# A hybrid transformer block on one core: the token's norm scale moved behind the input projections, and x loaded in three column pieces

## The reference, cut to what matters

```
h    = x * rsqrt(mean(x*x over channels) + 1e-6) * g_pre_mix     # 256 x 2048
proj = h @ w_in                                                  # 2048 x 20496
m_qk, m_v, m_o, m_if, a_q, a_k, a_v, merge = split(proj)
m_qk = silu(causal_conv4(m_qk) ); gates from m_if + b_gates      # mLSTM branch
attention over a_q, a_k, a_v (ALiBi, block-causal)               # attention branch
mix  = (sigmoid(merge_m) * y_m + sigmoid(merge_a) * y_a) @ w_out
x    = x + rmsnorm(mix);   then an FFN with w_up, conv3, gelu, w_down, and a last norm
```

## Time and profile before

| what | us |
|---|---|
| median of 3 runs | 1852.43 |
| lowest, highest | 1851.65, 1852.64 |
| profiled execution: span, first to last instruction | 1850.7 |
| TensorE busy in it | 1836.6 |
| VectorE, ScalarE, GpSimd busy in it | 1116.1, 899.2, 66.6 |

### The profile page before, as it was taken

The page is one execution under the profiler, slowest core; times in us unless marked ns, Lnnn a source line. Parts: engine busy times, 40 slices in busy tenths (PEclk is TensorE's granted clock), DMA queues, the critical chain, the costliest instruction groups (busy, mean ns, idle before and its releaser), DMA issues.

```text
span 1850.7 us, 35627 instructions
## 1 busy us (share of the span) xinstructions
PE 1836.6 (99%) x13864; PEld 1745.0 (94%) x13864; DVE 1116.1 (60%) x1340; ACT 899.2 (49%) x1174; POOL 66.6 (4%) x92
## 2 busy tenths in 40 slices
PE   8999999999999999999999999999999999999998
PEld 8999999999999999999999889999999999988886
DVE  6666556645665566545555557766667667755555
ACT  6554445444454455444434446555555555544443
POOL 2800000000000000000000000000000000000000
PEclk9999999999999999999999999999999999999999
DMA  7665666566656665666666754666666666665554
GB/s 241 194 192 175 191 182 177 177 188 181 178 172 192 179 176 177 188 193 193 192 192 196 253 198 149 194 193 194 193 193 193 192 194 190 196 215 193 194 193 143
DMA packets 164514, 351.44 MB, mean 190 GB/s; under 512 B 10937, under 2 KB 11473, under 8 KB 163793
## 3 DMA queue, kind: packets, MB, share of 16 engines
q1 hardware_dynamic: 162784, 344.11, 61.1%
q10 hardware_dynamic: 1280, 5.08, 0.7%
q0 software_dynamic: 368, 1.09, 0.2%
HBM read 348.12 MB, written 2.12 MB: 189 GB/s over the span
## 4 chain that ended last, share of the span: by engine, by line
PE 97%; issue 1%; DVE 1%; DMA 1%; ACT 0%; POOL 0%; DVEq 0%; POOLq 0%; SPq 0%; ACTq 0%
PE ps L1348 26%; PE ps L1347 26%; PE ps L1346 26%; PE ps L1563 11%; PE ps L1567 6%; PE ps L1523 1%; PE ps L1427 0%; PE ps L1499 0%; PE ps L1384 0%; DMA gm<-in_channel_rows 0%; DMA raw<-in_w_out 0%; PE ps L1500 0%; ACT ha_hi L631 0%; DVE x L926 0%; PE ps L1506 0%
## 5 line engine op out<-in xcount | busy, mean ns | idle before, releaser
L930 DVE TENSOR_TENSOR w_lo<-raw,w_hi 128x1024 fp32r<-128x1024 f32 x637 | 777.6, 1226 | 640.3 <-ACT w_hi L593 638.2
L593 ACT ACTIVATE w_hi<-raw 128x1024 fp32r<-128x1024 f32 (+1 forms) x641 | 677.7, 1060 | 767.1 <-PE ps L1348 606.9
L1346 PE MATMUL ps<-h,w_hi 128*128 128x256 f32 x3200 | 885.7, 277 | 0.2
L1348 PE MATMUL ps<-h,w_lo 128*128 128x256 f32 x3200 | 884.1, 276 | 0.0
L1347 PE MATMUL ps<-h,w_hi 128*128 128x256 f32 x3200 | 884.1, 276 | 0.0
L1346 PEld LDWEIGHTS ps<-h,w_hi 128*128 128x128 f32 x3200 | 600.9, 188 | 0.9 <-issue 0.6
L1347 PEld LDWEIGHTS ps<-h,w_hi 128*128 128x128 f32 x3200 | 600.8, 188 | 0.3
L1348 PEld LDWEIGHTS ps<-h,w_lo 128*128 128x128 f32 x3200 | 600.7, 188 | 0.0
L1563 PE MATMUL ps<-w_hi,ks_hi 128*128 128x512 f32 x448 | 174.5, 389 | 0.0
L1567 PE MATMUL ps<-w_lo,ks_hi 128*128 128x512 f32 x448 | 174.3, 389 | 0.0
L1563 PE MATMUL ps<-w_hi,ks_lo 128*128 128x512 f32 x448 | 138.1, 389 | 0.0
(11 more groups left out here) (180 smaller groups left out, 1432.4 us busy)
## 6 DMA issues: line engine op xcount, KB each, us to landing
raw<-in_w_in SPq DMA_DIRECT2D x287, 512.0 KB, 3.7
raw<-in_w_up SPq DMA_DIRECT2D x176, 512.0 KB, 4.4
raw<-in_w_down SPq DMA_DIRECT2D x88, 512.0 KB, 4.5
raw<-in_w_branch_m SPq DMA_DIRECT2D x32, 512.0 KB, 4.5
raw<-in_w_branch_a SPq DMA_DIRECT2D x32, 512.0 KB, 4.6
raw<-in_w_out SPq DMA_DIRECT2D x32, 512.0 KB, 4.7
x<-in_x ACTq DMA_DIRECT2D x1, 2048.0 KB, 12.5
gm<-in_channel_rows SPq DMA_DIRECT2D x2, 512.0 KB, 4.6
```

The lines of the kernel that those rows point to most:

```text
L593: return nc.scalar.activation(out_ap, in_ap, ACT.Copy, scale=scale)
L930: nc.vector.tensor_tensor(w_lo[:, at:at + UNIT], raw[:, slot, :], w_hi[:, at:at + UNIT].bitcast(F32), ALU.subtract).then_inc(lo_done, 1)
L1346: nc.tensor.matmul(out_ap, stat_hi, mov_hi, start=start, stop=False, skip_group_check=True)
L1348: return nc.tensor.matmul(out_ap, stat_lo, mov_hi, start=False, stop=stop, skip_group_check=True)
```

## The change

The scale is no longer applied to x. x is loaded in three column pieces of 2, 6 and 8 k-tiles, each with all 256 tokens (256, 768 and 1024 KB), and these loads alternate with the first weight units. TensorE transposes the 128x128 blocks through the identity as before, but of x as it was loaded, with no scale on it. The products of w_in are those of x times gain, and every reader of a w_in chunk multiplies by the token's scale. For channel-major results this is a row of 256 scales, which is made as a product on TensorE (`scales_by_token`) and kept as `rs_row`; for token-major results (v) it is a scalar per partition.

```diff
-            for i in range(len(ROW_PIECES)):
-                sp.dma_start(row_piece(gm_rows, i), x_pieces[i]).then_inc(x_loaded[i], 16)
-            sp.dma_start(wif_flat, by_channel[:, C_ALL:C_ALL + KT * 2 * HEADS]).then_inc(wif_loaded, 16)
+            load_x(0)
             for k, done in ((0, first_loaded), (1, raw_loaded[0])):
                 ...
+            for u in range(1, RING):
+                if u < len(X_PIECES):
+                    load_x(u)
+                load(BASE_MIX + u, u, chunk_unit(u, w_in_v, A_Q))
+            sp.dma_start(wif_flat, by_channel[:, C_ALL:C_ALL + KT * 2 * HEADS]).then_inc(wif_loaded, 16)
```

ScalarE, start and first turn (the identity now comes with the first channel constants, 144 columns):

```diff
-            for i in range(len(ROW_PIECES)):
-                scalar.wait_ge(x_loaded[i], 16)
-                squares(...)
-            ...
-            norm_tiles(0, C_GPM, {1: ..., 4: ..., 6: ..., 12: ...})
+            scalar.wait_ge(chan_loaded, 16)
+            early_tile(0)
+            ...
+            split_first(0, first_hi)
+            early_tile(1)
+            split_first(512, hi_done)
+            early_tile(2)
+            early_tile(3)
+            for u in range(1, RING):
+                split(0, u, u, away(u))
+                if u < 3:
+                    early_tile(2 * u + 2)
+                    early_tile(2 * u + 3)
+            early_steps = {2: lambda: row_squares(0, 0), 3: lambda: row_squares(1, 0), 4: lambda: row_squares(0, 1),
+                           5: lambda: row_squares(1, 1), 6: wif_high, 9: scale_rows, 10: gate_rows}
...
+                    if first and 2 <= u < 6:
+                        early_tile(2 * u + 4)
+                        early_tile(2 * u + 5)
+                    if first and u in early_steps:
+                        early_steps[u]()
-                    if first and u == 5:
+                    if first and u == 11:
                         gate_exponents()
-                    if u == 7:
-                        copy(qT[:], banks(0, 2, T)).then_inc(read_act, 1)
-                    if u == 15:
-                        copy(kT[:], banks(2, 2, T)).then_inc(read_act, 1)
```

VectorE (the same order of tiles and splits, then):

```diff
+            def by_token(out_ap, pair, done_unit, read):
+
+                vec.wait_ge(pe_done, done_unit)
+                nc.vector.tensor_tensor(out_ap, tiles_of(pair), rs_tiles, ALU.mult).then_inc(read, 1)
+            early_steps = {6: row_sums, 7: wif_parts, 8: repeat_scales, 9: lambda_dots, 10: rows_known, 12: lambda_full}
...
+                    if u == (10 if first else 7):
+                        by_token(qT[:], 0, g * U_MIX + units_done(7), read_qk)
+                    if first and u == 10:
                         gate_sums()
+                    if u == 15:
+                        by_token(kT[:], 1, g * U_MIX + units_done(u), read_qk)
-                    if u in (31, 33, 39, 41):
+                    if u in (31, 39):
+                        by_token(scaled, 1 if u == 31 else 0, g * U_MIX + units_done(u), read_dve)
+                    if u in (32, 33, 40, 41):
+                    if u == 55:
+                        by_token(og[:], 0, g * U_MIX + units_done(u), read_og)
+                    if u == 63:
+                        by_token(gm[:, ds(g * 4, 4), :], 1, g * U_MIX + units_done(u), read_gm)
```

TensorE:

```diff
-            for i in range(18):
-                nc.tensor.transpose(ps[:, 0, 0:P], ident, ident)
-            ...
-            again(gm_rows, 6, FIRST)
+            pe.wait_ge(zero_tile, 1)
+            for i in range(6):
+                nc.tensor.matmul(ps[:, 0, 0:P], zeros, zeros, start=True, stop=True)
+            def scales_by_token():
+
+                pe.wait_ge(rs_rep, 1)
+                for b in range(TB):
+                    last = nc.tensor.matmul(ps[:, 6, b * P:(b + 1) * P], rs_reps[:, b * P:(b + 1) * P], ident, start=True, stop=True)
+                last.then_inc(rs_psum, 1)
+            pe.wait_ge(chan_loaded, 16)
+            early_tiles(0)
+            early_tiles(1)
...
+                    if g == 0 and u < UNITS_CHUNK:
+                        if u == 0:
+                            first_products()
+                        for kk in range(1 if u == 0 else 0, 2):
+                            ready(u)
+                            pe.wait_ge(h_done, 2 * u + kk + 1)
+                            unit_channels(u, 0, h_hi, h_lo, range(kk, kk + 1))
+                        for pair in ((2, 3), (4,), (5,), (6,), (7,))[u] if u < 5 else ():
+                            early_tiles(pair)
                         continue
+                    if g == 0 and u == 8:
+                        scales_by_token()
+                        gates()
```

More of the change, by code:

```diff
@@ L148, in channel_rows @@
 def channel_rows(a):
[L151 to L154, removed]
+    gate_bias = np.zeros((2, P), np.float32)
+    gate_bias[0, 0:HEADS] = a["b_gates"][0, 0:HEADS]
+    gate_bias[1, 0:HEADS] = a["b_gates"][0, HEADS:]
+    rows = [np.eye(P, dtype=np.float32)]
+    rows += [a[n].reshape(-1, P) for n in ("g_pre_mix", "m_head_norm", "a_head_norm", "g_pre_ffn")]
     rows += [gate_bias] + [a[n].reshape(-1, P) for n in ("m_conv_w", "m_conv_b", "ffn_conv_w", "ffn_conv_b")]
@@ L157, in channel_rows @@
     by_channel = np.concatenate([np.concatenate(rows).T, gates], axis=1)
-    x_pieces = [a["x"][0][b * P:(b + 1) * P, c0:c0 + n] for b, c0, n in ROW_PIECES]
+    tiles = a["x"][0].reshape(TB, P, KT, P).transpose(1, 2, 0, 3)
+    x_pieces = [tiles[:, k0:k1] for k0, k1 in X_PIECES]
     return np.ascontiguousarray(np.concatenate([m.ravel() for m in (by_channel, *x_pieces)]).reshape(P, -1))
@@ L1047, in _, with tiles_of, conv_taps @@
             flat = prob[:].rearrange("p a b -> p (a b)")
[L1049 removed]
+            scaled = flat[:, 0:4 * T].rearrange("p (t c) -> p t c", c=T)
+            def tiles_of(pair):
+                return ps[:, 2 * pair:2 * pair + 2, :].rearrange("p b (t c) -> p (b t) c", c=T)
+            def by_token(out_ap, pair, done_unit, read):
+                vec.wait_ge(pe_done, done_unit)
+                nc.vector.tensor_tensor(out_ap, tiles_of(pair), rs_tiles, ALU.mult).then_inc(read, 1)
+            def conv_taps(g, src, dst, tiles, taps, first_tile, weight, stride):
                 for j in range(1, taps):
@@ new lines, in _, with early_tiles @@
+            for i in range(6):
+                nc.tensor.matmul(ps[:, 0, 0:P], zeros, zeros, start=True, stop=True)
+            def early_tiles(pair):
+                for i in range(len(X_PIECES)):
+                    if X_PIECES[i][0] == 2 * pair:
+                        pe.wait_ge(x_loaded[i], 16)
+                for k in (2 * pair, 2 * pair + 1):
+                    for b in range(TB):
+                        ins = nc.tensor.transpose(early_place(k)[:, b * P:(b + 1) * P], gm[:, k, b * P:(b + 1) * P], ident)
+                    if ends_group(k):
+                        ins.then_inc(h_psum, 1)
@@ new lines, in first_products, with place @@
+            def first_products():
+                a_hi, a_lo = h_hi[:, 0, :], h_lo[:, 0, :]
+                def place(t):
+                    return ps[:, t // 2, t % 2 * T:t % 2 * T + T], slice(away(0) + t * P, away(0) + (t + 1) * P)
+                pe.wait_ge(first_hi, 1)
+                pe.wait_ge(h_hi_done, 1)
+                for t in range(4):
+                    out_ap, c = place(t)
+                    nc.tensor.matmul(out_ap, w_hi[:, c], a_hi, start=t % 2 == 0, stop=False, skip_group_check=True)
+                pe.wait_ge(h_done, 1)
+                for t in range(4):
+                    out_ap, c = place(t)
+                    nc.tensor.matmul(out_ap, w_hi[:, c], a_lo, start=False, stop=False, skip_group_check=True)
+                pe.wait_ge(first_lo, 1)
+                for t in range(4):
+                    out_ap, c = place(t)
+                    nc.tensor.matmul(out_ap, w_lo[:, c], a_hi, start=False, stop=False, skip_group_check=True)
@@ new lines, in gates @@
+            def gates():
+                pe.wait_ge(wif_ready, 1)
+                for k in range(KT):
+                    nc.tensor.matmul(ps[:, 7, 0:T], hm_hi[:, k, 0:P], h_hi[:, k, :], start=k == 0, stop=False,
+                                     skip_group_check=True)
+                    last = nc.tensor.matmul(ps[:, 7, 0:T], hm_hi[:, k, 0:P], h_lo[:, k, :], start=False, stop=k == KT - 1,
+                                            skip_group_check=True)
+                last.then_inc(gates_psum, 1)
```

300 lines of the change are left out of this document (156 added, 144 removed).

## The result

| what | before | after |
|---|---|---|
| median, us | 1852.34 | 1861.18 |
| lowest, highest | 1851.65, 1852.64 | 1859.74, 1863.50 |
| profiled execution: span | 1850.7 | 1861.7 |
| its last matmul starts | 1843.4 | 1854.3 |

Four executions of each kernel were taken. The changed kernel is slower: ratio 1.0049, 95% interval 1.0036 to 1.0063. The forecast was 1854.3 in a range up to 1858.5; the result lies 2.7 us above that end.

A forecast was written before the change was run, and what follows sets the result against it. TensorE, busy 99% of the span, was taken to bound the kernel; -0.5 + 1.3 + 1.1 = +1.9 us gave span 1852.6 and median 1854.3 us, range 1851.0 to 1858.5.

The forecast's parts named there:

- The first product: Start of unit 0: x piece 1 lands at 7.45, so TensorE's first product starts at 7.9, 4.8 us earlier.
- Unit 2 and the extra products: TensorE before unit 8: a 0.4 us wait for unit 2's weights, +0.4 for transposes, +0.4 for the scales' products.
- The new wait at unit 8: Ahead of `scales_by_token`, TensorE idles 3.0 us until ScalarE and VectorE finish unit 11's split and the scales are repeated.
- head and clock: Stretch up to the scales at unit 8, 40.3 against 40.9, taken as -0.5 us, plus +1.3 for the start's clock.
- The clock: Start: TensorE may still run at 1.2 GHz when products begin; +1.3 us, bounds 0 and 3.
- the fall behind the stop at unit 8: Rival: the clock falls in the wait at unit 8 and returns after 3.5 us; 1.75 us more, 1856.0; chance 0.10.
- the gates come later, and GpSimd's cover runs out: First turn, units 33 to 37: later gates delay GpSimd's chain and root, making VectorE late; +1.1 us, bounds 0 and 4.
- the first rival: "GpSimd's chain decides", u = 29 to 37, first turn: chain 3 us longer beside VectorE's softmax, 1857.3 us; chance 0.18.
- The 28 whole-pair readings: New scaled readings on VectorE, 34 us of work, covered by the ring's spare time; cost 0 in all turns.

The follow-up runs named there:

- e1: Changed kernel with TensorE making the scales and the 32 gate products behind unit 8 instead of ahead of it: 1856.38 us, ratio 1.0024 against the kernel before.
- e5: Changed kernel with 13 more identity transposes at the start, between the tiles of x piece 0 and those of piece 1: 1861.16 us, ratio 1.0047.
- e10: Changed kernel with six of the eight running-maximum rounds of GpSimd's gate chain left out, so its output is not the gates: 1856.06 us, ratio 1.0020.
- e7: Changed kernel with the edits of e1, e2 and e5 together: 1851.94 us, ratio 0.9999 against the kernel before.
- e4: Changed kernel with 26 identity transposes added to fill TensorE's stop at unit 8: 1860.25 us, ratio 1.0044 against the kernel before.
- e2: Changed kernel with GpSimd's first attention root put ahead of the gate's stores and gathers: 1856.38 us, ratio 1.0022 against the kernel before.
- e3: Changed kernel with a semaphore in place of the drain in the first turn's attention root, its place kept: 1856.73 us, ratio 1.0024.
- e6: Kernel before, with only the gate's rows, sums and exponents and the two lambda steps moved to where the changed kernel has them: 1853.68 us, ratio 1.0008.
- e9: e8 with GpSimd's gate chain waiting ahead of its fifth running-maximum round for both softmax results: 1849.44 us, ratio 0.9985 against the kernel before.
- e8: e7 with x in four pieces of 2, 2, 4 and 8 tiles and 6 filling transposes: 1850.89 us, ratio 0.9995 against the kernel before.

## Why the prediction was wrong

The profiled span was summed to 1852.6 and came out at 1861.7. Of the 9.1 us between them:

- **The first product** was put at 7.9 and started at 9.51: +1.6. In the profiled executions of e1 to e5 and e10, with the same pieces, it started at 7.92 to 8.26. So the step was right within 0.4, and this one execution was unlucky by 1.3 us or more.
- **Unit 2 and the extra products.** In e7 one start comes 0.71 behind the last at 15.1, so the wait of 0.4 was 0.6 there. In the changed kernel, whose start was late, there was none, but in e1 to e5 and e10, which start as early as e7, there was no more than 0.2 either. So the wait came in full in one profiled execution of eight.
- **The new wait at unit 8** was put at 3.0: it is 2.86 idle, 3.02 more from start to start. Right, also in its place and releaser. The sum of head and clock said +0.8 behind it; the kernels that stand still here have +1.4 (e5) to +3.7 (after) at the column 52.9, e4, where the stop is filled, has +0.8, and e1 without it has -1.9. (By its own terms the head was 40.3 against 40.9, -0.6 and not -0.5.)
- **The clock.** +1.3 for the start came near the truth in the profiled execution: eleven starts 0.21 apart, 0.09 too long each, and two more that are longer, 1.2 in all, in a low stretch of 8.9 to 12.3. There the clock fell behind a stop, where the forecast had it not yet risen. But the fall behind the stop at unit 8 was a rival with 0.10, at 1.75 us: it measured 1.6 in the profile, and came in four of the five profiled executions with the stop, not in e2. And I had put no stop and so no fall at unit 33: 1.7 more. These are the rival's mechanism and its price twice over; the chance was too low. How long the slow stretch at the start lasts also differs: the first product was followed by 7 starts 0.21 us apart in e1, 11 in the changed kernel and 20 in e2, whose programs for TensorE are the same up to there. The Trainium skill ("TensorE: Matmul & The Clock Gate", "Part 1: The HAM clock gate") says that the number of slow matmuls at the start differs from run to run of the same kernel, and these counts agree.
- **The step that failed: "the gates come later, and GpSimd's cover runs out", +1.1, bounds 0 and 4.** I had the chain start 19.6 us later and the root at 112.1. The chain started 22.5 later (the late first product and the fall at unit 8 are in that), ran 45.6 us to its first store in place of 44.7, and the root came at 120.8. (`gate_sums` has six small instructions, not eight; they took the 2.8 us that I had.) Its drain I had at the price of before, 0.83, from a row where no DMA was under way. Behind the gathers it was 5.46 us. That is the term that was mis-sized: the stop at unit 33 cost 3.7 and the fall behind it 1.7, so 5.4 for 1.1. e2 and e3 take this wait away, each by another edit, and bring 4.8 and 4.5 us of the medians; e6 shows that the drain alone costs next to nothing (0.4 us) while the root still comes by 114.
- **A stop I did not have: 1.6 us in the softmax near 93.** I had seen that the chain would now run beside VectorE's softmax, and had counted only what this does to GpSimd (the first rival: 3 us longer). It was 0.8 us longer (the 45.6 and 44.7 above); it was VectorE that paid, 1.60 for 0.75 and 3.43 for 2.35 us, and its results were what TensorE waited for. The Trainium skill ("SBUF — State Buffer", "SBUF: two separate sides") has a VectorE instruction with two SBUF inputs and a GpSimd one that reads SBUF lock each other out, whichever starts first; by e9 the trace agrees (1.60 and 0.75 us for the same pair), and the cost was on the side that I left out.
- **The 28 whole-pair readings** cost 0, within 0.2 us here and 0.8 in any run: the lateness is +10.7 at 119 and +10.9 at 1598. Right.

In sum, for the 9.1: 1.6 (start) + 1.6 (clock at unit 8) + 1.6 (softmax) + 4.3 (unit 33: 5.4 for 1.1) = 9.1. That it comes out to the tenth is luck: at the column 52.9 the kernel is 2.9 us later than forecast, not 3.2, and 0.3 more are spread behind 119. The nearest rival, "GpSimd's chain decides", had the place (u = 29 of the first turn) and the direction, but not the mechanism. The range was too narrow: its upper end, 1858.5, is about what both upper bounds give together (+3 and +4 in place of +1.3 and +1.1: 1858.9), with no room for a rival on top or for a stop that was not in the sum.

What stays open: what decides whether a stop of 3 us is followed by a fall of the clock (eight of nine at units 8 and 33 were, in the profiles); why this execution's first product came 1.3 us late; and why the median of e5 did not follow its start.

## What to carry to other kernels

When an edit delays the input of a helper engine's chain, go through that engine's whole queue, its own transfers included: what stood alone before now stands behind outstanding DMAs, and a drain there waits for them. Where two engines slow each other, as VectorE and GpSimd do here, look at both, and first at the one whose result is needed soonest. A pause in a chain whose result had some 30 us of slack bought 1.4 us; a new stop of 3 us on TensorE cost nearly 5 here (4.8, e1).

## What the runs showed of the hardware

- A drain on GpSimd lasts until its own outstanding DMAs are done: 5.46 (after), 5.53 (e1), 6.15 (e4), 5.47 (e5) and 6.62 us (e6), each ending 0.47 to 0.48 us behind the landing of the last gather. Where the gathers had landed before the root it took 0.83 us (before, e10), where none had been issued 0.14 (e2, e9), and a semaphore in its place, with the gathers still running, 0.08 (e3).
- The same pair of VectorE instructions took 0.75 us while GpSimd waited (e9) and 1.60 beside its chain (e8); two splits 2.35 and 3.43.
- Behind a stop of some 3 us at unit 8 or 33 TensorE is at 1.2 GHz for 3.4 us in eight of nine cases (0.51; after, e1, e3, e4, e5, e10) and at 2.4 GHz in one (1.00, e2); each such stretch costs 1.5 to 1.7 us.
